# Moving the squares, sums, norm products and scan products of a hybrid decoder's first part off GpSimd

## What is computed

```python
h = rmsnorm(x, g_mix)                # x * rsqrt(mean(x*x) + eps) * g
z = h @ w_in                         # 1024 -> 2560 columns
xa, ga, q, k, v = split(z)
xa_c = causal_dwconv(concat[conv_hist, xa])        # width 4
r, gi = sigmoid(block_diag(xa_c, w_r)), sigmoid(block_diag(xa_c, w_i))
a = exp(-8 * r * softplus(-lam))
u = sqrt(1 - a*a) * (gi * xa_c)
hs = scan(a, u)                      # h[t] = a[t] * h[t-1] + u[t]
ya = hs * gelu(ga)
q, k = partial_rope(q), partial_rope(k)
```

## Time and profile before

| | |
|---|---|
| median of 3 runs | 2858.26 us (2856.94 to 2859.93) |
| the profiled execution's own time | 2854.36 us |
| its span in the profile | 2852.7 us |
| first part (to the last tile of the fifth chunk) | 0 to 551.7 us of the span |
| PE busy over the span | 2702.9 us (95%) |
| DVE busy | 2129.0 us (75%) |
| ACT busy | 1500.5 us (53%) |
| POOL busy | 861.9 us (30%) |

### The profile page before, as it was taken

How to read it: one execution, slowest core, us unless ns; L and a number is a source line. 1 busy time by engine, 2 the same in 40 slices (tenths; PEclk the granted TensorE clock), 3 DMA queues, 4 the chain that set the end, 5 groups by cost and what they waited for, 6 DMA issues and landing times.

```text
span 2852.7 us, 44188 instructions
## 1 busy us (share of the span) xinstructions
PE 2702.9 (95%) x15584; PEld 2579.0 (90%) x15584; DVE 2129.0 (75%) x3696; ACT 1500.5 (53%) x2903; POOL 861.9 (30%) x872
## 2 busy tenths in 40 slices
PE   8999999899999999969999899998999989999998
PEld 7898899867788989969999899998999989999997
DVE  7988988688645767888888888888888755465463
ACT  6656666656677753335555555555555444233231
POOL 4677776545201436650020101000000012122121
PEclk9999999899999999989999999999999999999999
DMA  5344344456554348844323242332432365456532
GB/s 168 127 145 154 118 158 145 142 190 195 185 194 159 114 125 292 285 160 161 110 90 112 87 141 98 107 112 80 154 112 99 108 240 214 164 185 232 171 112 93
DMA packets 189079, 430.42 MB, mean 151 GB/s; under 512 B 20980, under 2 KB 111988, under 8 KB 184772
## 3 DMA queue, kind: packets, MB, share of 16 engines
q1 hardware_dynamic: 145312, 367.55, 38.1%
q10 hardware_dynamic: 39396, 43.10, 4.7%
q0 software_dynamic: 4160, 17.04, 1.6%
HBM read 350.47 MB, written 77.17 MB: 150 GB/s over the span
## 4 chain that ended last, share of the span: by engine, by line
PE 69%; DVE 13%; POOL 4%; ACT 4%; issue 4%; DMA 4%; ACTq 0%; DVEq 0%; SPq 0%; POOLq 0%
PE bank L2277 10%; PE bank L2279 10%; PE bank L2278 10%; PE bank L2015 8%; PE bank L2016 8%; PE bank L2017 8%; PE bank L2088 7%; PE bank L2113 2%; PE bank L2100 2%; DVE w_lo L1176 2%; POOL sq L1742 1%; PE bank L2112 1%; DVE d L1311 1%; DMA normed_rows<-x 1%; POOL ssq L1744 1%
## 5 line engine op out<-in xcount | busy, mean ns | idle before, releaser
L2277 PE MATMUL bank<-b_hi,w_hi 128*128 128x348 f32 x2016 | 659.3, 327 | 54.0 <-ACT u2s L1064 28.9
L2279 PE MATMUL bank<-b_hi,w_lo 128*128 128x348 f32 x2016 | 654.9, 325 | 0.0
L2278 PE MATMUL bank<-b_lo,w_hi 128*128 128x348 f32 x2016 | 653.9, 324 | 0.0
L2277 PEld LDWEIGHTS bank<-b_hi,w_hi 128*128 128x128 f32 x2016 | 385.0, 191 | 58.3 <-issue 29.5
L2278 PEld LDWEIGHTS bank<-b_lo,w_hi 128*128 128x128 f32 x2016 | 385.3, 191 | 0.4 <-issue 0.4
L2279 PEld LDWEIGHTS bank<-b_hi,w_lo 128*128 128x128 f32 x2016 | 384.6, 191 | 0.0
L2015 PE MATMUL bank<-ff_hi,w_hi 128*128 128x416 f32 x960 | 340.1, 354 | 8.9 <-DVE w_lo L1692 8.9
L2016 PE MATMUL bank<-ff_lo,w_hi 128*128 128x416 f32 x960 | 337.1, 351 | 0.0
L2017 PE MATMUL bank<-ff_hi,w_lo 128*128 128x416 f32 x960 | 335.2, 349 | 0.0
L2015 PE MATMUL bank<-h_hi,w_hi 128*128 128x416 f32 x800 | 292.0, 365 | 24.6 <-DVE h_lo L1189 24.5
L1125 ACT ACTIVATE w_hi<-stage 128x1024 fp32r<-128x1024 f32 x120 | 126.8, 1059 | 354.1 <-PE bank L2017 341.3
(11 more groups left out here) (280 smaller groups left out, 5966.1 us busy)
## 6 DMA issues: line engine op xcount, KB each, us to landing
stage<-in_w SPq DMA_DIRECT2D x404, 512.0 KB, 3.4
past<-in_past SPq DMA_DIRECT2D x32, 1152.0 KB, 6.8
ff_in<-gated_rows SPq DMA_DIRECT2D x15, 1664.0 KB, 9.6
gated_rows<-ucb SPq DMA_DIRECT2D x72, 174.0 KB, 1.9
vb<-out_v SPq DMA_DIRECT2D x48, 256.0 KB, 3.0
attention_rows<-ob SPq DMA_DIRECT2D x32, 264.0 KB, 2.1
oc<-attention_rows SPq DMA_DIRECT2D x16, 528.0 KB, 4.0
hp<-normed_rows SPq DMA_DIRECT2D x3, 2784.0 KB, 12.1
```

The source lines that it names most:

```text
L2277: e.matmul(out, hi, b_hi[j][:, kb], start=begins and kb == 0, stop=False, skip_group_check=True)
L2278: e.matmul(out, hi, b_lo[j][:, kb], start=False, stop=False, skip_group_check=True)
L2279: last = e.matmul(out, lo, b_hi[j][:, kb], start=False, stop=kb == KH - 1, skip_group_check=True)
```

## The change

All of it is in the first part. ACT squares the pieces of the next chunk (`square_a`), the first one at t = 4 straight into the sum `ssq`, then one at each of t = 4 to 10 into the one buffer `sq`. DVE adds `sq` to the sum (`add_square`), one at each of t = 5 to 11, each behind the low half of that step. ACT's square k waits for the sum of piece k - 1, since both use `sq`. The 8 norm products go to DVE, two at each of t = 13 to 16. The products d * r and gi * d move from POOL into DVE's `scan`, right ahead of the scan. POOL keeps `gate_y`, the rotation and gi * xc, 6 of its operations for a group.

```diff
@@ scalar
+            def square_a(c, k):
+                if k == 0:
+                    e.wait_ge(xt_loaded, 16 * c)
+                    e.wait_ge(ms_ready, c)
+                elif k == 1:
+                    if not (isinstance(c, int) and c == 1):
+                        e.wait_ge(sq_step, (KD - 1) * (c - 1))
+                else:
+                    e.wait_ge(sq_step, (KD - 1) * (c - 1) + k - 1)
+                e.activation((sq if k else ssq)[:], xT[:, k], ACT.Square).then_inc(sq0_ready, 1)
+
+            def squares_a(c, t):
+                if t == 4:
+                    square_a(c + 1, 0)
+                if 4 <= t < 3 + KD:
+                    square_a(c + 1, t - 3)
...
-            def ahead(c, t):
+            def ahead(c, t, more):
                 split_hi(c * W_IN + t + AHEAD, (t + AHEAD) % RING)
+                if more:
+                    squares_a(c, t)
@@ vector
             def scan(c, first, j):
                 m = JT * c + j
+                e.wait_ge(s_ready, m + 1)
+                e.tensor_tensor(d_[j % 2][:], d_[j % 2][:], r_[:], ALU.mult).then_inc(sd_ready, 1)
+                e.wait_ge(sd_ready, m + 1)
+                e.wait_ge(u1_ready, m + 1)
+                e.tensor_tensor(gi[:], gi[:], d_[j % 2][:], ALU.mult).then_inc(u_ready, 1)
...
+            def add_square(c, k):
+                e.wait_ge(sq0_ready, KD * c + k + 1)
+                if k > 1:
+                    e.wait_ge(sq_step, (KD - 1) * (c - 1) + k - 1)
+                e.tensor_tensor(ssq[:], ssq[:], sq[:], ALU.add).then_inc(sq_step, 1)
+
+            def prepare(c, t):
+                if 5 <= t < 4 + KD:
+                    add_square(c + 1, t - 4)
+                if t == 13:
+                    e.wait_ge(rstd_ready, c + 2)
+                if 13 <= t < 17:
+                    norm_scale(range(2 * t - 26, 2 * t - 24))
...
                     ahead(c, x_a)
+                    if more:
+                        prepare(c, x_a)
...
@@ gpsimd
-            def square_sum(c, ks):
...
-            def norm_scale(ks):
...
-                    if more and j < 2:
-                        square_sum(c + 1, range(KD)[4 * j:4 * j + 4])
...
-                    if more and j == 3:
-                        norm_scale(range(4, KD))
...
-                        if i == 0 and j == 2 and more:
-                            e.wait_ge(rstd_ready, c + 2)
-                            norm_scale(range(4))
...
                     e.tensor_tensor(gi[:], gi[:], xc[j % 2][:], ALU.mult).then_inc(u1_ready, 1)
-                    e.wait_ge(s_ready, m + 1)
-                    e.wait_ge(lru_a, m + 1)
-                    e.tensor_tensor(d_[j % 2][:], d_[j % 2][:], r_[:], ALU.mult).then_inc(sd_ready, 1)
-                    e.wait_ge(sd_ready, m + 1)
-                    e.wait_ge(u1_ready, m + 1)
-                    e.tensor_tensor(gi[:], gi[:], d_[j % 2][:], ALU.mult).then_inc(u_ready, 1)
@@ tensor
             def mean_square(c):
-                e.wait_ge(sq_step, (2 * KD - 1) * c)
+                e.wait_ge(sq_step, (KD - 1) * c)
                 e.wait_ge(rms_ready, c)
```

More of the change, by code:

```diff
@@ L747, in chunk @@
                     x_a, g_a, qk, v_t = 5 * j, 5 * j + 1, (5 * j + 2, 5 * j + 3), 5 * j + 4
-                    ahead(c, x_a)
+                    ahead(c, x_a, more)
                     if not first:
@@ L778, in chunk @@
                         store_v(m - 1, c if j else c - 1, (j - 1) % JT)
-                    ahead(c, g_a)
+                    ahead(c, g_a, more)
                     e.wait_ge(taps, 3 * m + 3)
@@ L797, in chunk @@
                     for i, t in enumerate(qk):
-                        ahead(c, t)
+                        ahead(c, t, more)
                         b = done(c, t)
@@ L803, in chunk @@
                         e.activation(raw[i][:], b[:, 0:C], ACT.Identity, scale=-SCALE if 2 * j + i < JT else 1.0).then_inc(evacuated[t % 4], 1)
-                    ahead(c, v_t)
+                    ahead(c, v_t, more)
                     next_first = j == 3 and more
@@ L1280, in chunk @@
                     ahead(c, g_a)
+                    if more:
+                        prepare(c, g_a)
                     e.wait_ge(xch_ready, m + 1)
@@ L1290, in chunk @@
                         ahead(c, t)
+                        if more:
+                            prepare(c, t)
                         if not (first and j == 0):
@@ L1303, in chunk @@
                     ahead(c, v_t)
+                    if more:
+                        prepare(c, v_t)
                     if j == 3 and more:
@@ L1729, in _ @@
         def _(e):
-            def square_sum(c, ks):
[L1732 to L1744, removed]
-            def norm_scale(ks):
-                for k in ks:
-                    e.tensor_tensor(xT[:, k], xT[:, k], rstd[:], ALU.mult).then_inc(hn_ready, 1)
             def store_ya(c, j):
```

## The result

The changed kernel takes 2873.11 us (median of 4 runs, 2872.51 to 2876.18), the kernel before 2857.60 beside it: ratio 1.0058 [1.0045, 1.0070], slower by 0.6%. The forecast of 2861 is 12 us too low; the range 2838 to 2879 holds the result. The profiled execution took 2872.51 us.

A forecast was written before the change was run, and what follows sets the result against it. PE, busy 95%, bounds the kernel. New losses of 5.5 + 3 + 2.4 = 10.9 us replace 10.1, 10.8 and 9.7 in chunks 1 to 3; with chunk 0 (+8.0) and the last (-7.5), +2.6 on 2858.26 gives 2861, range 2838 to 2879.

The forecast's parts named there:

- chain to the seventh sum: To-and-fro between ACT and DVE after tile 3: 45.1 us against PE's 39.4, taken as a 5.5 us wait before meetings.
- low clock behind the mean square: After PE's mid-chunk stop of 8.5 us the clock runs lower for some us, costing 2.4 us a chunk.
- meetings: Six DVE operations on the way to the seventh sum coincide with POOL's: 3 us a chunk, ends 0 and 6.3.
- The `v_cols` waits of before go as well: Inside a chunk: PE's waits for `v_cols`, which stood behind POOL's squares, disappear.
- The loss at the border goes: Between chunks: DVE needs 30 us from step 12 against PE's 39, so `h_lo` no longer holds PE up.
- Chunk 0: First chunk: a new loss of 11.7 us in place of 3.7, +8.0.
- Last chunk: Chunk 4, without mean square and sums: its loss goes, -7.5 us, and it takes 97 us.
- Taps of 2.0 us: DVE's three taps take 2.0 us, instead of 3.55 beside POOL's d * r.
- The lock: Rival: every meeting costs DVE a whole POOL operation, 6.3 us a chunk instead of 3; 2874 us, chance 0.25.
- The hidden chain: Rival: sums come as early as the order allows, PE loses under 1 us at the mean square; 2820 us, chance 0.10.
- Squares with their own table: Rival: ACT's squares need four table loads of 1.28 us in each chunk; 2881 us, chance 0.04.
- Borders as before: Rival: DVE is no earlier, some 8.5 us stay at each of four borders on top of the sum; 2895 us, chance 0.06.

## Why the prediction was right or wrong

Its mechanism was right for the middle of the chunk, which the chain to and fro between ACT and DVE sets. The border's loss shrinks and the last chunk gains, but not for the reason it gave. Two terms of the sum were too small. Chunk 2 lost 112.7 - 97.7 = 15.0 us where the forecast had 10.9:

| part of chunk 2 | forecast | measured | from |
|---|---|---|---|
| border | 0 | 2.2 | tile 3 ends at 267.19, 20.7 behind the border; 18.5 by the prediction's numbers, 18.8 where nothing stops PE there (`h_lo` first) |
| chain to the seventh sum, less PE's 39.4 | 8.5 | 10.1 | from 267.19 to the mean square at 316.65 |
| low clock behind the mean square | 2.4 | 2.6 | 316.65 to 359.17 is 42.5; 39.9 with sums on GpSimd (297.75 to 337.62) |

*The chain.* Forecast 45.1 us plus 3 of meetings from the end of tile 3 to the seventh sum; measured 316.60 - 267.19 = 49.4. The tanh came 5.5 us after tile 3, as forecast. Meetings cost 4.0: three sums at 1.48 instead of 0.58, and the first step of d at 1.25 and 0.81 instead of 0.38. PE took the wait in two stops, not in one of 6 to 11 us. That square and sigmoids stand ahead of `v_cols` was in the chain's working, but not that PE needs `v_cols` before it comes to the sum. So the prediction's "The `v_cols` waits of before go as well" failed: POOL's squares no longer hold `v_cols` up, but the squares in ACT's own list now do. By this reckoning the first stop costs nothing of its own, since PE would have stood longer at the second without it, nor does the low clock between the two; no run tried that apart.

*The border* is the step that failed: "The loss at the border goes." DVE has not 30 us from step 12 on but 35 with its meetings (34.6 with sums on GpSimd), and it doesn't begin when PE does. Where it begins decides. In chunk 2 of the four kernels with squares and sums on POOL, the kernel before among them, step 12 begins 9.1 or 9.2 us behind tile 12; in those with them on ACT and DVE it is 2.5 to 3.1. From the border behind that chunk to the end of tile 3 PE then takes 25.8 to 26.8 us in the former and 19.0 to 21.3 in the latter, wherever the norm products are. Moved alone these changed nothing: DVE's time from step 12 to `h_lo` grew by them from 31.6 to 35.0 us.

Why DVE is late with the sums on POOL stands in the traces. ACT's sigmoids wait for `gate_y`, and that stands in POOL's list behind the squares. ACT in the kernel before, then POOL, ACT and DVE with sums on GpSimd, all at the first sigmoids of chunk 2:

```profile
266.03 1.28 ACT L813 ACT_TABLE_LOAD   x1 [5.88 <-POOL d L1774]
```

```profile
263.85 1.09 POOL L1814 TENSOR_TENSOR d<-r_,gl 128x416 f32<-128x416 f32 x1
265.03 1.28 ACT L832 ACT_TABLE_LOAD   x1 [5.06 <-POOL d L1814]
268.10 1.75 DVE L1354 TENSOR_SCALAR d<-r_ 128x416 f32<-128x416 f32 x1 [6.12 <-ACT r_ L837]
```

The prediction put `h_lo`'s lateness down to the norm's last products and to meetings, and left this wait out. It is read from the traces; no run moved `gate_y` alone. In the changed kernel step 12 begins 2.5 us behind tile 12 (317.57), and DVE reaches `h_lo` at 358.95, PE the border at 359.17. The new stop at the mean square is not what brings that: with two buffers PE stands there for 0.29 us, step 12 is 3.0 us behind tile 12 (284.89), and the border's stop is as short. DVE's step 12 in the changed kernel, then with two buffers:

```profile
320.09 1.72 DVE L1197 TENSOR_TENSOR w_lo<-stage,w_hi 128x1024 fp32r<-128x1024 f32 x1 [0.47 <-ACT w_hi L682]
```

```profile
287.85 1.72 DVE L1197 TENSOR_TENSOR w_lo<-stage,w_hi 128x1024 fp32r<-128x1024 f32 x1 [0.47 <-ACT w_hi L682]
```

What is left of the stop, 1.2 to 2.2 us at each of four borders, is the last low half ahead of `h_lo`, made longer by POOL: with it behind, the stops behind chunks 1 to 3 are gone.

*The other terms.* Chunk 0: +8.0 forecast, +8.4 measured. Last chunk: -7.5 and -5.1, the border again (99.4 instead of 96.9). Taps of 2.0 us: 2.03 measured. Over all, chunks 1 to 3 are 6.0, 4.1 and 4.1 us worse than forecast, with the last chunk's 2.4 and chunk 0's 0.4 together 17: 2.6 forecast, 19.6 measured. The four borders make up some 11 of the 17 (22.4, 20.7, 20.8 and 20.8 us to the end of tile 3 instead of 18.5), and the range had been widened for the chain, the meetings and the clock alone: that it holds the result is in part luck.

*The rivals.* The lock would have given 2874, and 2873 was measured, but not for its reason: DVE's meetings on the chain cost 4.0 us and not 6.3, a third of the difference in a chunk. The single rows bear it out, however. POOL's timeline of the changed kernel beside the sum at 295.16:

```profile
294.22 1.97 POOL L1817 TENSOR_TENSOR sh<-sh,rope 128x416 f32<-128x416 f32 x1 [2.81 <-DVE sh L1345]
```

DVE's low half ran from 294.03 to 295.24 at its usual 1.21; POOL's product, begun inside it, took 0.9 us more than its 1.08; and the sum, begun inside that one, took 0.9 more than its 0.58. The Trainium skill's page SBUF — State Buffer, section "Who interferes with whom", says that who issues first has the shared ports for the whole instruction; these rows agree. In these rows DVE pays only where it comes second, and only for what is left of POOL's operation. Not all rows are so plain: the low half at 269.47 began 0.3 us ahead of POOL's next operation and took 3.63. The hidden chain is refuted for the changed kernel, but it is what two buffers bring: 2827.5 measured, 2820 reckoned. Squares with their own table: no load stands ahead of a square. Borders as before: refuted in the changed kernel, and just what happens with sums on GpSimd.

## What to carry to other kernels

Where two engines hand one buffer to and fro, look at what stands behind the waiting instruction in each list: work that is short on both engines becomes a chain in lock step, and a second buffer or a place behind the urgent instruction frees it. Here that one wait turned 1.0% gained into 0.6% lost. Ask of an engine that should "be early" when it begins, not only how much it has to do; and try the parts of a change one by one, for one part here lost more than the others could gain.

## What had not been expected of the hardware

Short stops left the clock alone. With two buffers PE stood 1.15 us at a border and the granted clock stayed 1.00 over the chunk; around stops of 3.62 and 4.61 us it was 0.80 and 0.74, and behind one of 2.15 us 0.62. The length of the stop alone does not decide: behind one of 2.22 us, at the first border with two buffers, it stayed 1.00. What does decide stays open. Three taps, forecast at 2 us, took 2.03 in all of chunk 2, while beside POOL's d * r they had taken 3.55: 1.5 us less for three taps, against the 1.2 that two scan products cost DVE.
